# A bias-table product moved into the warm-up, and a first weight tile taken by halves, in a two-layer encoder trunk

## The reference, cut to what matters

```
def swiglu_ffn(x, w_up, w_down):
    gate, up = jnp.split(x @ w_up, 2, axis=-1)      # w_up 1024 x 5632
    return (jax.nn.silu(gate) * up) @ w_down        # w_down 2816 x 1024
...
logits = logits + bias_tab[t5_bucket(sel - qpos[None, :, None])]   # rel_bias, 32 buckets x 8 heads
...
for l in range(DEPTH):
    x = layer_norm(ALPHA * x + 0.5 * swiglu_ffn(x, ffn1_w_up[l], ffn1_w_down[l]), ...)
    x = layer_norm(ALPHA * x + hybrid_mixer(x, ...), ...)
    x = layer_norm(ALPHA * x + 0.5 * swiglu_ffn(x, ffn2_w_up[l], ffn2_w_down[l]), ...)
```

## Time and profile before

| | |
|---|---|
| median of 3 executions | 1135.23 us (1134.87 to 1135.81) |
| the profiled execution | 1134.67 us, of which the span from first to last instruction is 1132.5 us |
| TensorE busy | 1121.6 us, 99% of the span |
| VectorE, ScalarE, GpSimd busy | 67%, 49%, 36% |
| memory read | 205.56 MB, 182 GB/s over the span |

### The profile page before, as it was taken

How to read it: one execution, slowest core, us unless ns; L and a number is a source line. 1 busy time by engine, 2 the same in 40 slices (tenths; PEclk the granted TensorE clock), 3 DMA queues, 4 the chain that set the end, 5 groups by cost and what they waited for, 6 DMA issues and landing times.

```text
span 1132.5 us, 17628 instructions
## 1 busy us (share of the span) xinstructions
PE 1121.6 (99%) x5916; PEld 924.1 (82%) x5916; DVE 763.9 (67%) x1078; ACT 557.1 (49%) x799; POOL 408.0 (36%) x567
## 2 busy tenths in 40 slices
PE   9999999999999999999999999999999999999997
PEld 7888888878788888888888888888777888888885
DVE  5657745889966866685586465468898687555544
ACT  5545433574673455453355454436846635454440
POOL 2889976107700378997700000011276000000001
PEclk9999999999999999999999999999999999999999
DMA  8866653644556585666367566536536466757541
GB/s 269 242 205 191 221 187 109 201 143 150 170 172 210 161 237 181 191 217 201 116 183 223 189 224 200 189 98 224 163 119 184 149 204 184 238 163 249 187 149 38
DMA packets 158719, 207.50 MB, mean 183 GB/s; under 512 B 13144, under 2 KB 107672, under 8 KB 158656
## 3 DMA queue, kind: packets, MB, share of 16 engines
q1 hardware_dynamic: 154928, 201.70, 55.5%
q10 hardware_dynamic: 2704, 3.36, 1.0%
q0 software_dynamic: 1024, 1.61, 0.8%
HBM read 205.56 MB, written 1.06 MB: 182 GB/s over the span
## 4 chain that ended last, share of the span: by engine, by line
PE 72%; POOL 18%; DVE 5%; issue 3%; DMA 1%; ACT 1%; SPq 0%; POOLq 0%; DVEq 0%; ACTq 0%
PE ps L718 22%; PE ps L720 21%; PE ps L719 21%; POOL small L1521 7%; POOL b_bar L1521 3%; DVE wlo L1180 2%; POOL tab_c L1521 2%; POOL tab_s L1657 1%; POOL tab_s L1521 1%; POOL tab_c L1654 1%; PE ps L1010 1%; PE ps L745 1%; DMA raw<-in_ffn_w_up 1%; PE ps L735 1%; PE ps L939 1%
## 5 line engine op out<-in xcount | busy, mean ns | idle before, releaser
L1180 DVE TENSOR_TENSOR wlo<-raw,whi 128x1024 fp32r<-128x1024 f32 (+1 forms) x372 | 485.1, 1324 | 187.6 <-ACT whi L410 174.1
L410 ACT CAST whi<-raw 128x1024 fp32r<-128x1024 f32 (+1 forms) x372 | 386.7, 1047 | 292.7 <-PE ps L720 228.5
L718 PE MATMUL ps<-whi,xh 128*128 128x512 f32 (+1 forms) x1056 | 417.9, 396 | 1.5 <-DVE wlo L1180 1.1
L720 PE MATMUL ps<-whi,xl 128*128 128x512 f32 (+1 forms) x1056 | 409.3, 388 | 0.0
L719 PE MATMUL ps<-wlo,xh 128*128 128x512 f32 (+1 forms) x1056 | 408.6, 387 | 0.0
L718 PEld LDWEIGHTS ps<-whi,xh 128*128 128x128 f32 x1056 | 198.4, 188 | 44.8 <-issue 3.6
L720 PEld LDWEIGHTS ps<-whi,xl 128*128 128x128 f32 x1056 | 198.2, 188 | 41.3
L719 PEld LDWEIGHTS ps<-wlo,xh 128*128 128x128 f32 x1056 | 198.6, 188 | 37.4
L1545 POOL TENSOR_TENSOR rstd<-var_eps,cst 128x1 f32<-128x1 f32 x12 | 18.2, 1519 | 529.5 <-DVE var_eps L1227 529.5
L718 PE MATMUL ps<-whi,hh 128*128 128x512 f32 x352 | 139.7, 397 | 0.0
L720 PE MATMUL ps<-whi,hl 128*128 128x512 f32 x352 | 137.3, 390 | 0.0
(11 more groups left out here) (185 smaller groups left out, 1089.8 us busy)
## 6 DMA issues: line engine op xcount, KB each, us to landing
raw<-in_ffn_w_up SPq DMA_DIRECT2D x352, 256.0 KB, 4.0
raw<-in_ffn_w_down SPq DMA_DIRECT2D x176, 256.0 KB, 3.0
raw<-in_w_in SPq DMA_DIRECT2D x128, 256.0 KB, 3.3
raw<-in_w_branch SPq DMA_DIRECT2D x32, 256.0 KB, 3.2
raw<-in_w_out SPq DMA_DIRECT2D x32, 256.0 KB, 4.3
bias_g<-bias_rows ACTq DMA_DIRECT2D x16, 192.0 KB, 3.9
raw<-in_w_in SPq DMA_DIRECT2D x16, 148.0 KB, 2.3
affine<-in_ln_g SPq DMA_DIRECT2D x4, 512.0 KB, 5.5
```

The lines of the kernel that those rows point to most:

```text
L410: nc.scalar.copy(whi[:, s % RING, 0:w], raw[:, s % RAW, 0:w]).then_inc(S["hi_done"], 1)
L718: nc.tensor.matmul(o, ah, bh, start=start, stop=False)
L720: return nc.tensor.matmul(o, al, bh, start=False, stop=stop)
L1180: nc.vector.tensor_tensor(wlo[:, s % RING, 0:w], raw[:, s % RAW, 0:w], f32(whi[:, s % RING, 0:w]), ALU.subtract).then_inc(S["split_done"], 1)
```

## The change

Three edits, all at the opening. The bias table product leaves `prepare_bank` and goes between the third and the last of what are now 4 warm-up products (there were 8). It now writes bank 3, and since bank 3 belongs to chunk 1's second token tile, a wait for `bias_copied` stands ahead of that pass. Weight tile 0 on token tile 0 is issued as the four products of its high part, which wait only for `hi_done`, and then the two of its low part, which wait for `split_done`; the transposes of token tile 1 follow them as before.

```
-                nc.scalar.copy(bias_sb[:, :], ps[0:N_HEADS, 6, :]).then_inc(S["bias_copied"], 1)
+                nc.scalar.copy(bias_sb[:, :], ps[0:N_HEADS, 3, :]).then_inc(S["bias_copied"], 1)
...
-            def prepare_bank(f, prep):
-                if f == 0:
-
-                    pe.wait_ge(S["const_landed"], 48)
-                    nc.tensor.matmul(ps[0:N_HEADS, 6, :], bias_tab[:, :], buckets[:, :], start=True, stop=True
-                                     ).then_inc(S["bias_done"], 1)
+            def bias_table():
+
+                pe.wait_ge(S["const_landed"], 48)
+                nc.tensor.matmul(ps[0:N_HEADS, 3, :], bias_tab[:, :], buckets[:, :], start=True, stop=True
+                                 ).then_inc(S["bias_done"], 1)
+
+            def prepare_bank(prep):
...
             def opening(prep):
 
-                for q, t in ((0, 0), (1, 0), (0, 1), (1, 1), (2, 0), (2, 1), (3, 0), (3, 1)):
+                pe.wait_ge(S["hi_done"], 1)
+                pe.wait_ge(S["x_ready"], part(0, 0, 0))
+                for k in range(2):
+                    for a in (xh, xl):
+                        nc.tensor.matmul(ps[:, 0, :], a[:, k, tok(0)], w(whi, 0, k * 512, k * 512 + 512),
+                                         start=k == 0 and a is xh, stop=False)
+                wait_split(0)
+                for k in range(2):
+                    nc.tensor.matmul(ps[:, 0, :], xh[:, k, tok(0)], w(wlo, 0, k * 512, k * 512 + 512),
+                                     start=False, stop=False)
+                x_transpose(0, 1)
+                for q, t in ((1, 0), (0, 1), (1, 1), (2, 0), (2, 1), (3, 0), (3, 1)):
...
-                    if (q, t) == (0, 0):
-                        x_transpose(0, 1)
-                prepare_bank(0, prep)
-                up_chunk(0, 0, 4, 1, 1, False)
+                prepare_bank(prep)
+                up_pass(0, 0, 4, 1, 1, 0, False)
+                pe.wait_ge(S["bias_copied"], 1)
+                up_pass(0, 0, 4, 1, 1, 1, False)
                 h_transpose(0, 0, 0, False)
...
-            warm_up(8)
+            warm_up(3)
+            bias_table()
+            warm_up(1)
```

More of the change, by code:

```diff
@@ L768, in up_pass, with up_chunk @@
                     ins.then_inc(S["up_done"], 1)
-            def up_chunk(i, f, s, c, b, wait_bank=True):
+            def up_chunk(i, f, s, c, b):
                 for t in range(NT):
-                    up_pass(i, f, s, c, b, t, wait_bank)
-            def prepare_bank(f, prep):
-                if f == 0:
-                    pe.wait_ge(S["const_landed"], 48)
-                    nc.tensor.matmul(ps[0:N_HEADS, 6, :], bias_tab[:, :], buckets[:, :], start=True, stop=True
-                                     ).then_inc(S["bias_done"], 1)
+                    up_pass(i, f, s, c, b, t)
+            def bias_table():
[3 more added lines that the diff above has]
+            def prepare_bank(prep):
                 if prep is not None:
@@ L810, in first_chunks @@
                 up_pass(0, f, s, 0, 0, 1, False, None, stage)
-                prepare_bank(f, prep)
+                prepare_bank(prep)
                 up_pass(0, f, s + 4, 1, 1, 1, False)
```

## The result

Against 1135.23 us of the kernel before (median of 13, 1133.90 to 1136.27) the changed kernel takes 1138.38 us (median of 13, 1135.37 to 1141.12): ratio 1.0025, 95% interval 1.0018 to 1.0033. It is slower, by 2.8 us as the ratio has it and by 3.2 us between the medians, and its executions spread over 5.7 us where those of before spread over 2.4. The traced execution took 1137.75 us with a span of 1135.7, 3.2 more than before.

The account below looks back on a forecast made before the run. TensorE, busy 99% of the span, was taken as the bound. Terms -0.8 - 0.9 + 3.1 + 0.1 - 0.2 = +1.3 us on 1134.67 gave 1136.0, forecast 1136.5 for the median; range 1134.6 to 1138.6.

Parts of the forecast that it names:

- a clock that falls for part of the stretch: Behind the bias copy wait, TensorE at half clock for part of 5.9 us: +1.3 + 2.1, setting the range's top, 1138.6.
- Opening: First weight tile by halves: products start before its low part is ready, then token tile 1's landing holds; -0.8 us.
- Bias product out of the bank preparation: Between chunk 0 and chunk 1: bias product gone, the small transpose of par stays; -0.9 us, between -0.8 and -1.1.
- The wait: Chunk 1's second token tile: TensorE waits for the bias copy from 26.4 to 29.5, 3.1 us.
- a sign against me: At ScalarE's copy of weight tile 7: a move of more than 1 us would show the prediction wrong.
- The wait of 0.2 us at its `b_bar`: TensorE's weight load at line 868, 141.9 us: its wait for GpSimd goes, giving back 0.2 us.
- the fourth rival: GpSimd's chain grows as operations turn slow beside VectorE's moved work; with four, +3.5 us, 1138.7; 5%.
- The third rival: No bias copy wait; GpSimd at 141.9 us takes 1.5 of the 1.7 gain: -0.3 to -0.7, 1134.7; 2%.
- the +1.3 of the sum: Whole kernel: two opening gains, bias copy wait, restart and GpSimd wait removed, no clock fall; +1.3 us.
- the forecast's own case: Opening gains outweighed by the bias copy wait, clock holding: +1.3 us, 1136.5; 70%.
- the likeliest case: Bias copy wait without a clock fall: +1.3 us, spanning 1134.7 to 1137.3; 70%.
- the clock rival: TensorE's clock falls during the bias copy wait, first products twice 0.23 apart: +4.2 us, 1139.4; 15%.

Follow-up runs that it names:

- e4: Kernel before with only the first weight tile taken by halves: 1134.52 us, ratio 1.0000.
- e1: Changed kernel with ScalarE's bias table copy and store moved early, between the copies of weight tile 1 and token tile 1: 1134.43 us, ratio 0.9993.
- e3: Changed kernel plus 12 zero products on TensorE just ahead of the wait for the bias copy: 1136.73 us, ratio 1.0011.
- e11: A further single execution of e8's kernel, with trace: 1136.84 us.
- e12: A second further single execution of e8's kernel, with trace: 1136.62 us.
- e2: As e1, and the first feed-forward's state-space parameter copy and clip put ahead of chunk 0's silu, starting GpSimd earlier: 1133.72 us, ratio 0.9984.
- e6: Changed kernel plus 6 zero products, half of e3's, ahead of the wait for the bias copy: 1138.73 us, ratio 1.0035.
- e5: Changed kernel without the first weight tile's new order, leaving only the bias product's move: 1138.26 us, ratio 1.0026.
- e9: A further single execution of e6's kernel, with trace: 1141.28 us.
- e10: A second further single execution of e6's kernel, with trace: 1140.63 us.
- e7: Kernel before with only e2's earlier state-space parameter copy and clip, so GpSimd starts earlier: 1134.68 us, ratio 0.9997.
- e8: e2's kernel without the first weight tile's new order: 1135.41 us, ratio 1.0000.

## Why the prediction was right, and where it was off

The measured time lies in the stated range, 0.2 us below its upper end and 1.9 above the forecast of 1136.5. It is 0.25% up, just beyond the 0.2% within which 0.79 of the chance lay. That it is in the range owes something to luck: the part of the range in which it lies was there for a clock that falls for part of the stretch, a case that had 15% even with the full fall. The mechanism that I made the ground of the forecast, that the change trades two gains for a wait on a copy queued behind weight tile 11, is what happened.

- *Opening.* First product 8.28 (8.5 said), transposes 9.95 (10.15), next product 10.80 (10.94), held by token tile 1's landing as said. The gain is 0.93, in e4 alone 0.64, where -0.8 was said. The wait for the bias parameters was not free: 0.4 us. They landed at 7.1, not 6.7, and the six warm-up passes ahead took 0.83 us in place of 1.3; it cost nothing further on.
- *Bias product out of the bank preparation.* Chunk 1 began at 20.48 (20.8 said). From chunk 0's last product it is 0.26 where I had left 0.23 + 0.25; the transpose of `par` costs almost nothing in front of a product. The term is -1.1, the end of the range given.
- *The wait.* TensorE there at 26.0 (26.4), copy ended at 29.13 (29.5), wait 3.0 (3.1). I had named a move of tile 7's copy by more than 1 us as a sign against me. It moved by 1.37 (0.64 by the split of tile 3, the rest by a faster transfer), but tile 11 came 4.3 us after tile 7's split in place of 3.8, and of the lead 0.86 was left at the bias copy.
- *GpSimd.* The wait of 0.2 us at its `b_bar` went, as said. Its start was 0.86 earlier (29.99, was 30.85), but its end 1.5 later (143.37). The chain grew, from 111.0 to 113.4 us, which the fourth rival had thought possible, and did not hold TensorE. The third rival took its end to follow its start alone, and e1 shows otherwise: there the copy ran early, GpSimd's start moved by 0.49 only, and TensorE lost 0.2 us, not 1.5.
- *The clock.* This is the term that was mis-sized. I gave 15% to a fall, for 2.9 us. In the trace it fell and cost 1.7, which the +1.3 of the sum did not have. Of 13 executions the mean clock was 0.998 in three, which took 1135.37, 1135.96 and 1136.06 us: that fits the forecast's own case, at +0.1 to +0.8 against +1.3. It was 0.997 or less in nine, 1137.45 to 1141.12. One, at 0.999, took 1138.58. The median belongs to the rival, not to the likeliest case. I had argued from the one gap in the trace, 0.84 us, that did no harm, and took 3.1 us once as "the short end"; no row bore out that harmlessness reaches so far. e3 prices the clock at 1138.38 - 1136.73 = 1.65 us. These are medians taken at two times, at which the kernel before took 1135.23 and 1135.24.

The Trainium skill ("TensorE: Matmul & The Clock Gate", section "HAM oscillation — how this bites in real kernels") tells of waits of several microseconds between bursts of products, each of which sends the clock back to half. By it I should have given the clock rival the larger part. The traces agree in kind (3.0 us in the changed kernel), and go further: gaps of 1.3 and 1.5 us were enough in e11 and e12.

## What to carry to other kernels

Before a wait is put on a small copy, read what stands ahead of that copy on its own engine, and what that waits for: here a table ready at 8 us was copied at 29 because of a weight stream. Move the copy together with the product (e1, e2), and look for the next engine that meets the one you made faster (in e2 ScalarE's `q_t`, 0.7 us). Do not take another engine's chain for a clock of its own: see whether its length stays when its start moves. An idle stretch of TensorE is to be priced twice, as the wait and as a lower clock behind it; where it can't be removed, zero products that fill most of it paid (e3, 1.6 us), and half as many did not (e6).

## What the runs showed of the hardware that was not expected

- The granted clock fell about or after the end of idles of 3.0 (changed kernel), 2.8 (e5), 2.3 and 1.8 (e9, at the bias copy and in layer 1), 1.9 (e10, in layer 1), 1.5 (e12) and 1.3 us (e11). It did not after 1.8 (e7, ahead of its first weight tile at 9.17), 1.7 (e8, at the same place), 1.65 and 1.4 (e6), 1.5 (e10, at the bias copy), 1.25 (e5, ahead of its first weight tile) and 1.2 us (e3). The length of the idle alone does not decide it.
- The fall came 0.7 us before TensorE's restart in e5 and 0.2 before it in e12, and 0.1 (e10), 0.25 (changed kernel), 0.3 (e11), 1.45 and 2.0 us (e9) after it. In e9 the first six products behind the wait for the bias copy began 0.23 to 0.34 apart, and the next ones 0.43.
- In the opening the profile's clock does not tell the level: in the trace of before it reads 1.00 from 2 us on, while the first transposes are 0.21 us apart and the later ones 0.10. There the pace has to be read.
- The slow stretch was 3.4 us long in the changed kernel, at both places in e9, and in e11 and e12, and 6.8 in e5 and at 853 us in e10.
- A mean granted clock of 0.997 or less goes with a longer execution in nearly every case, those of the kernel before included: of the 33 beside e5 to e8 one took 1140.72 us at 0.995, two 1136.25 and 1137.64 at 0.997, and of the 33 beside e1 to e4 one took 1138.46 at 0.996. The rest had 0.998 or 0.999, which the idle end of the span explains. None of the four has a trace, so where the kernel before loses its clock is not known. The changed kernel's 1138.58 at 0.999 is an exception that I can't explain.
- GpSimd's operations of one kind (128x128, two operands) took 0.40 to 0.46 us or 1.3 to 1.5. In the trace of before those that ran between 133.08 and 138.55 are slow, and VectorE was making `wlo` from 132.97 to 138.33; the last one (140.41) is slow beside another `wlo` (140.30 to 141.53). So a longer or earlier chain does not end where its start would say. In the traces that wait for its end (before, e1, e4) it ended 0.05 us ahead of TensorE's weight load; in all the others it ended 1.2 us ahead of the transposes (1.7 in e8), with starts from 23.0 to 31.2. That VectorE sets the pace is read off these coincidences; no run tests it.
